# The first conditioning vector as 16 columns: weights stationary, the vector moving, the last two chunks fetched behind all rows of x

## The reference, cut to what matters

```
x = layer_norm(x, ln_in_g, ln_in_b)
c_act = silu(c)                         # c: 1024 numbers
mod = c_act @ w_ada + b_ada             # w_ada: 1024 x 6144, so 25 MB in float32
sh1, sc1, gt1, sh2, sc2, gt2 = split(mod, 6)
h = x * (1 + sc1) + sh1
proj = h @ w_in
```

## Time and profile before

| | us |
|---|---|
| median of 3 runs | 2986.38 (2985.26 to 2989.28) |
| the profiled execution | 2987.43 |
| its span, first to last instruction | 2985.3 |
| TensorE busy | 2835.7 (95% of the span) |
| first matmul of the program starts at | 12.46 |
| first matmul of the first projection starts at | 47.19 |

### The profile page before, as it was taken

The page is one execution under the profiler, slowest core; times in us unless marked ns, Lnnn a source line. Parts: engine busy times, 40 slices in busy tenths (PEclk is TensorE's granted clock), DMA queues, the critical chain, the costliest instruction groups (busy, mean ns, idle before and its releaser), DMA issues.

```text
span 2985.3 us, 33001 instructions
## 1 busy us (share of the span) xinstructions
PE 2835.7 (95%) x13226; PEld 2141.4 (72%) x13226; DVE 1804.8 (60%) x2633; ACT 1185.1 (40%) x1819; POOL 404.8 (14%) x246
## 2 busy tenths in 40 slices
PE   8999898999999999999999999998989799999998
PEld 3445576777888888886455877777777688887877
DVE  5786556557444544447256435733333589999998
ACT  3101544323211112225234336614332377777775
POOL 1022400004000000004000000000000137333332
PEclk9999999999999999999999999999999899999999
DMA  9320100012111111114000121110011699999996
GB/s 333 113 69 17 67 1 1 29 30 84 44 43 55 57 43 57 43 30 169 1 1 29 43 106 37 71 43 29 1 38 59 243 348 368 387 384 379 382 378 256
DMA packets 120512, 363.13 MB, mean 122 GB/s; under 512 B 14538, under 2 KB 48616, under 8 KB 95776
## 3 DMA queue, kind: packets, MB, share of 16 engines
q1 hardware_dynamic: 104096, 331.24, 30.2%
q0 software_dynamic: 16256, 29.71, 2.7%
HBM read 356.69 MB, written 29.38 MB: 129 GB/s over the span
## 4 chain that ended last, share of the span: by engine, by line
PE 69%; DMA 12%; DVE 10%; ACT 6%; issue 3%; POOL 1%; SPq 0%; POOLq 0%; DVEq 0%; ACTq 0%
PE PS L181 63%; PE PS L192 4%; DMA MR<-in_w_e_up 4%; DMA MR<-in_w_e_down 4%; DMA MR<-in_w_e_gate 3%; DVE ML L3127 2%; PE PS L591 1%; ACT MH L3122 1%; DVE BIG L847 1%; DMA BC<-xz,ST 1%; DMA XR<-in_w_e_down 1%; DVE ST L509 1%; DVE ST L1175 0%; ACT BIG L970 0%; DVE XR L1621 0%
## 5 line engine op out<-in xcount | busy, mean ns | idle before, releaser
L181 PE MATMUL PS<-BIG 128*128 128x512 f32 (+11 forms) x2384 | 603.7, 426 | 27.0 <-ACT BIG L839 5.6
L181 PEld LDWEIGHTS PS<-BIG 128*128 128x128 f32 (+4 forms) x2384 | 323.0, 187 | 251.2 <-issue 214.4
L3127 DVE TENSOR_TENSOR ML<-MR,MH 128x2048 fp32r<-128x2048 f32 x144 | 330.1, 2303 | 28.3 <-ACT MH L3122 27.9
L181 PE MATMUL PS<-MH,MX 128*128 128x512 f32 x1024 | 322.5, 396 | 12.0 <-DVE ML L3127 9.9
L3122 ACT CAST MH<-MR 128x2048 fp32r<-128x2048 f32 x144 | 275.4, 1914 | 93.5 <-DMA MR<-in_w_e_up 46.2
L181 PEld LDWEIGHTS PS<-MH,MX 128*128 128x128 f32 x1024 | 190.3, 190 | 56.6 <-DVE ML L3127 16.7
L181 PE MATMUL PS<-FWH,FHH 128*128 128x512 f32 x512 | 200.0, 391 | 4.4 <-DVE XR L1634 1.9
L181 PE MATMUL PS<-FXH,FWH 128*128 128x512 f32 x512 | 200.2, 391 | 1.1 <-DVE FWL L1486 1.1
L181 PE MATMUL PS<-ML,MX 128*128 128x512 f32 x512 | 200.5, 392 | 0.0
L181 PE MATMUL PS<-FXH,FWL 128*128 128x512 f32 x512 | 199.9, 390 | 0.0
L181 PE MATMUL PS<-FXL,FWH 128*128 128x512 f32 x512 | 199.7, 390 | 0.0
(11 more groups left out here) (498 smaller groups left out, 5395.8 us busy)
## 6 DMA issues: line engine op xcount, KB each, us to landing
MR<-in_w_e_gate SPq DMA_DIRECT2D x50, 1024.0 KB, 19.4
MR<-in_w_e_up SPq DMA_DIRECT2D x48, 1024.0 KB, 21.2
MR<-in_w_e_down SPq DMA_DIRECT2D x46, 1024.0 KB, 19.6
FWR<-in_w_ff SPq DMA_DIRECT2D x32, 1024.0 KB
XR<-in_w_e_down SPq DMA_DIRECT2D x18, 1024.0 KB
BC<-in_w_ada SPq DMA_DIRECT2D x32, 512.0 KB
XR<-in_w_e_up SPq DMA_DIRECT2D x16, 1024.0 KB
XR<-in_w_e_gate SPq DMA_DIRECT2D x14, 1024.0 KB
```

The lines of the kernel that those rows point to most:

```text
L181: ins = pe.matmul(o, l, r, start=(start and n == 0), stop=(stop and n == len(pairs) - 1), skip_group_check=True)
L3127: dve.tensor_tensor(cut_at(ML, i), raw(i), cut_at(MH, i).bitcast(F32), ALU.subtract).then_inc(e.w_lo.up(), 1)
```

## The change

All four chunks go the same way: `pe_mod_chunk(n)` takes 128x128 pieces of w_ada as the stationary operand and one column of silu(c), 128x1, as the moving one. Eight matmuls add up one column of 128 results, and four such groups fill the four columns of a chunk directly. The row copies on ScalarE, the turns of the rows on TensorE and VectorE's weighted sum for chunk 3 are gone. SyncE fetches row tiles 4 and 5 ahead of chunk 1 and row tiles 6 and 7 ahead of chunk 2. VectorE's bias add now waits for the fourth chunk's matmuls, and so does the fetch of the second retention weight.

```diff
             sp.dma_start(CT[:, 0:CST1], cst[:, 0:CST1]).then_inc(cst_in.up(), 16)
+            sp_x(4, 6)
             sp.dma_start(*ADA_SLOT[1]).then_inc(ada_in[1].up(), 16)
-            sp_x(4, 6)
+            sp_x(6, 8)
             sp.dma_start(*ADA_SLOT[2]).then_inc(ada_in[2].up(), 16)
-            sp_x(6, 8)
             sp.dma_start(*ADA_SLOT[3]).then_inc(ada_in[3].up(), 16)
...
         def act_mod():
             for t in range(4):
                 act_ln_std(t, ln_var, ln_std)
-            act_mod_row(0)
             act_x_evict(0)
             act_ln_std(4, ln_var, ln_std)
             act_ln_std(5, ln_var, ln_std)
-            act_mod_row(1)
             act_ln_std(6, ln_var, ln_std)
             act_ln_std(7, ln_var, ln_std)
-            act_mod_row(2)
             act_x_evict(1)
...
             P.wait_ge(*cs_ok[1])
             P.wait_ge(*ada_in[n][1])
-            if n >= 2:
-                P.wait_ge(*mod_row[n - 1])
-            mm(PS[0:1, 4 + n % 2, :], [(cs[:, k:k + 1], ADA_SLOT[n][0][:, k, :]) for k in range(8)]).then_inc(mod_mm.up(), 1)
-
-        def pe_mod_turn(n):
-            P.wait_ge(*mod_row[n + 1])
             for u in range(4):
-                ins = tr(PS[:, 6, 4 * n + u:4 * n + u + 1], MROW[:, n % 2, 128 * u:128 * u + 128])
-            ins.then_inc(mod_tr.up(), 1)
+                ins = mm(PS[:, 6, 4 * n + u:4 * n + u + 1],
+                         [(ADA_SLOT[n][0][:, k, 128 * u:128 * u + 128], cs[:, k:k + 1]) for k in range(8)])
+            ins.then_inc(mod_mm.up(), 1)
...
             for n in range(8):
                 pe_x_turn(n)
             pe_mod_chunk(1)
-            pe_mod_turn(0)
             pe_setup()
             pe_mod_chunk(2)
-            pe_mod_turn(1)
             for n in range(8, 12):
                 pe_x_turn(n)
-            pe_mod_turn(2)
+            pe_mod_chunk(3)
             for n in range(12, 16):
                 pe_x_turn(n)
-            P.wait_ge(*mod_acc[8])
-            for u in range(4):
-                ins = mm(PS[:, 6, 12 + u:13 + u], [(MACC[:, 128 * u:128 * u + 128], C("one")[:, 0:1])])
-            ins.then_inc(mod_tr.up(), 1)
...
             dve_cols()
-            V.wait_ge(*ada_in[3][1])
-            V.wait_ge(*cs_ok[1])
-            for k in range(8):
-                dve_weighted(MACC, ADA_SLOT[3][0][:, k, :], k, mod_acc, mod_acc.last)
-            V.wait_ge(*mod_tr[4])
+            V.wait_ge(*vs.last)
+            V.wait_ge(*cols_ok[1])
+            V.wait_ge(*mod_mm[4])
             dve.tensor_tensor(MODT[:, 0:16], PS[:, 6, 0:16], BCOLS, ALU.add).then_inc(mod_ok.up(), 1)
...
             S.wait_ge(*mod_mm[3])
             sp.dma_start(*WQK).then_inc(rqk_in.up(), 16)
-            S.wait_ge(*mod_acc[8])
+            S.wait_ge(*mod_mm[4])
             sp.dma_start(*WV).then_inc(rv_in.up(), 16)
```

More of the change, by code:

```diff
@@ L403, in program @@
         GT1, GT2 = bc(0), bc(1)
[L404 to L407, removed]
+        mod_mm, mod_ok = by_pe("mod_mm"), by_dve("mod_ok")
         ln_var, ln_done, ln_std = by_dve("ln_var"), by_dve("ln_done"), by_act("ln_std")
@@ L421, in act_ln_std @@
             act.activation(rst[:, t:t + 1], mv[:, t, 1:2], ACT.Sqrt, bias=epsc[:, 0:1]).then_inc(std.up(), 1)
-        def act_mod_row(n):
-            A.wait_ge(*mod_mm[n + 1])
-            if n >= 2:
-                A.wait_ge(*mod_tr[n - 1])
-            act.copy(MROW[:, n % 2, :], PS[0:1, 4 + n % 2, :]).then_inc(mod_row.up(), 1)
         def act_x_evict(th):
@@ L564, in program @@
         bank[0], bank[1], bank[2], bank[3] = fm_ev[13], fm_ev[14], fm_ev[15], fm_ev[16]
-        bank[4], bank[5], bank[6], bank[7] = mod_row[3], mod_row[2], mod_ok[1], cols_ok[1]
-        close(cols_pe, posr_ok, lam_ok, le_ok, ce_ok, mod_acc)
+        bank[6], bank[7] = mod_ok[1], cols_ok[1]
+        close(cols_pe, posr_ok, lam_ok, le_ok, ce_ok)
         w_in = X["w_in"][0]
@@ L1730, in program @@
         close(x1_mul, ln2_var, ln2_done, ln2_std, um_sq, um_std, x1_ok, x0_ok)
-        close(mod_mm, mod_tr, mod_row, mod_ok, mod2_tr, fm_ev, gt_in, modr_in)
+        close(mod_mm, mod_ok, mod2_tr, fm_ev, gt_in, modr_in)
         close(*fw_in, l1g_in, l1b_in, l2g_in, l2b_in)
```

## The result

The changed kernel takes 3017.5 us (median of 4 runs, 3014.03 to 3020.1) against 2987.83 us before (4 runs beside it): a ratio of 1.0098 (95% interval 1.0086 to 1.011), 26 to 33 us slower. The profiled execution took 3019.69 us, 32.3 more than the one before; its span is 3017.6.

The account below looks back on a forecast made before the run. TensorE's list, busy 95% of the span, was taken to bound the kernel. Half clock throughout +36.7, a longer low projection start +1.3, and clock returns -7.5 made +30, 3016.4 us; range 3002 to 3027, the forecast's own 3009 to 3021.

Parts of the forecast that it names:

- A chunk at full clock costs what it did: TensorE's w_ada chunks: 64 one-column passes at 0.111 us make 7.1 us, against 6.96 before, 0.1 more.
- the shift at full clock: First projection's start if all four chunks ran at full clock: 52.8 instead of 47.19, 5.6 us later.
- A pass at the low level: One-column passes and transposes on TensorE at half clock: 0.215 us each taken, between 0.198 and 0.248.
- The clock falls on narrow passes: Four chunks: one-column passes don't keep full clock; chunk 0 stays low, later chunks lose it; 26.6 us of the forecast.
- rival 2: Four chunks: weight loads count as clock work, full clock rises in chunk 0 and holds; +3.9 to +5.6 us; chance 0.10.
- Transposes raise it: Groups of 32 and 16 transposes on TensorE bring full clock back for stretches, giving about 7.5 us back.
- rival 1: TensorE before the projection: transposes hold the clock but don't raise it, half clock throughout; +38, 3024; chance 0.15.
- rival 3: Chunks 1 to 3: first transposes raise the clock, one-column passes then hold it; projection at 59.3, +12, 2998; chance 0.05.
- Two such stretches of 2 to 5 us make about 7.5 back: Returns to full clock during and after transposes on TensorE, each saving its own length: 7.5 us off +38.
- It then also starts low and stays so somewhat longer: First projection's start: low clock lasting longer than the present 3.4 us; +1.3, the mean of none and 2.6.
- The half-clock sum: TensorE's list wholly at half clock: 256 passes and 67 transposes at 0.215 us, projection at 83.9, +36.7 us.
- Hidden parts: Fetch order, SyncE's later waits, VectorE's and ScalarE's removed work: worth nothing, beyond 1.3 us for turns and row-copy wait.

Follow-up runs that it names:

- the run with zeros ahead: Changed kernel, one moving column, with eight extra matmuls of 512 columns of zeros on TensorE ahead of chunk 0; 3012.57 us in one run.

## Why the prediction was right

**The median**: +30 was forecast and +29.7 measured. So close a match is in part luck. The profiled execution has +32.3, terms of the sum were off in both directions (below), and the four runs of the changed kernel lie 6 us apart. The longest has a mean granted clock of 0.975 and the shortest 0.979; that fits returns of the clock that differ from one execution to the next, as the run with zeros ahead had one more than the changed kernel's profile, but the other three runs left no trace that shows it.

**A chunk at full clock costs what it did.** Forecast 0.111 us a pass from the eight passes in the earlier trace rows. With 64 moving columns a chunk took 7.09 us in the chain, 0.111 a pass, and with 128 it took 7.15, against 6.96 before. Right, and so is the shift at full clock: 5.6 was forecast, and with 128 columns it was 5.9.

**A pass at the low level.** Taken 0.215 between 0.198 and 0.248, from the earlier trace rows; measured 13.78/64 = 0.215 over all of chunk 0 with its first latency, and 0.213 in between. Right, and the bound of 0.111, a load that doesn't follow the clock, is ruled out.

**The clock falls on narrow passes.** This was the disputed step, read from one stretch late in the program in which TensorE was also idle for 30% of the time, so that stretch alone didn't separate the two. The falls at 35.08 in the changed kernel and at 32.27 in the run with zeros ahead, with no idle time before them, show it; the runs with 64 and 128 columns show that the moved columns are the cause. (The columns written to PSUM grow with them, and no run separates the two.) The rule that loads count as work for the clock (rival 2) is refuted by 13.7 us of back-to-back loads at 0.50.

**Transposes raise it** (rival 1 denied that). They did, at 31.67 in the changed kernel, and also with 64 columns (30.89), with chunk 3 on VectorE (63.2) and with zeros ahead (28.86). The Trainium skill, TensorE: Matmul & The Clock Gate, in its part on the PE-mode transpose, says full clock does not engage for transposes; for these float32 transposes of 128 columns, back to back, the traces differ: the rise at 31.67 comes after 5.60 us of transposes alone, and at full clock 32 of them took 3.49 us in the chain of the run with 128 columns, where they took 6.27, mostly at half clock, in the changed kernel. By that rule the median would have been 3024.

**A clock once up falls again** (rival 3 said that it holds): it did, at 35.08. With 64 columns rival 3 is just what happens, and its first projection, put at 59.3, came at 59.48.

**What was mis-sized.** Three terms, by +4.4, -1.3 and -0.9 us, which leaves +2.2. "Two such stretches of 2 to 5 us make about 7.5 back": there was one return, 3.4 us long, and it gave an estimated 3.1: 3.41/0.111 = 31 instructions, which at 0.212 each would have taken 6.5. By adding that back to 79.9, half clock throughout would have been 83.0. In the run with zeros ahead there were two such returns of 3.41 us before the last transposes; so it is the number of returns that this sum had wrong for the profiled execution. "It then also starts low and stays so somewhat longer", +1.3: the projection was low for 3.0 us (79.90 to 82.87), against 3.4 before, so nothing; no run shows the 2.6 us that its upper case stood for. The half-clock sum of +36.7 came to +35.8: the pass was 0.213 and not 0.215, and from the end of TensorE's list to the projection it took 1.7 and not 2.0. The sum was 36.7 + 1.3 - 7.5 = 30.5 against 35.8 + 0 - 3.1 = 32.7 in the trace.

**Hidden parts.** The order of fetches, SyncE's later waits, and VectorE's and ScalarE's lost work were put at nothing: the first is shown by its own run; for the others there is the agreement of 32.7 at the projection with 32.5 at 104.00 and 32.3 at the end, with differences of 2 to 3 us in between, so a small price of theirs isn't ruled out. The turns and the wait on the row copy were put at 1.3; in the chain of the run with chunk 3 on VectorE and 128 columns the pieces that held them are 1.5 shorter.

## What to carry to other kernels

When a matrix times one vector goes to TensorE, compare both forms by the pass and not by the multiplications: here 64 passes that load 128 columns and move one (7.1 us at full clock) cost as much as 16 passes that move 512 (6.96), and the form with the wide moving operand keeps the clock. If weights must be stationary, moving copies of the vector left a pass at 0.111 to 0.115 us at full clock, with 64 and with 128 columns, and 128 bought back 27 us. Look at the granted clock beside the busy share, and where no record of the clock exists yet, at the spacing of like instructions; and ask, before moving work from an engine that the chain never shows, what it could gain.

## What the runs showed of the hardware that was not expected

The clock fell during unbroken work on passes with one moving column: at 35.08 in the changed kernel, with TensorE and its loads busy for all of the 3.41 us before the fall and the 8.24 us behind it.

The same passes can fail to raise the clock and still hold it: dense passes of 64 moving columns stayed low for the 13.9 us of chunk 0, and once the transposes had raised the clock it stood at 1.00 through 14.4 us of them (chunks 1 and 2, with three set-up transposes between), and through chunk 3.

Matmuls of zeros, begun at 1.45 us, raised the clock too, at 5.0, 7.15 and 7.41 us in three runs. In the last of them it fell again at 14.23, after 2.8 us in which TensorE was idle.

A float32 pass with a 128-column load takes 0.111 to 0.112 us whether it moves 1, 64 or 128 columns at 2.4 GHz, the last by a moving operand of 128 copies read from one column.
